# Input and forget gate columns with the weights stationary and the tokens moving

## What is computed

```python
h = rms_norm_2(x, mix_norm[l])
z = h @ w_in[l] + b_in[l]
a_q, a_k, a_v, m_q, m_k, m_v, m_o, m_i, m_f, g_pre = jnp.split(z, SPLIT_POINTS, axis=-1)
...
hm = mlstm_chunkwise(mq, mk, mv,
                     softcap(m_i.astype(jnp.float32)), softcap(m_f.astype(jnp.float32)))
```

## Time and profile before

| | us |
|---|---|
| median of 3 runs | 1102.63 |
| lowest, highest | 1102.37, 1106.66 |
| the profiled execution's own time | 1103.3 |
| its span, first to last instruction | 1101.6 |
| TensorE busy in it | 1040.7 (94%) |
| VectorE, ScalarE busy | 556.0 (50%), 428.2 (39%) |
| mean granted TensorE clock | 0.979 |

### The profile page before, as it was taken

One profiled execution on the slowest core, in us unless ns is written; L12 is line 12 of the kernel. 1 busy time (PEld: TensorE's weight loads), 2 busy tenths in 40 slices (PEclk: granted clock), 3 DMA queues, 4 the chain that ended last, 5 costly groups with the idle time before them and its releaser, 6 DMA issues.

```text
span 1101.6 us, 13370 instructions
## 1 busy us (share of the span) xinstructions
PE 1040.7 (94%) x5377; PEld 799.0 (73%) x5377; DVE 556.0 (50%) x844; ACT 428.2 (39%) x564; POOL 51.5 (5%) x57
## 2 busy tenths in 40 slices
PE   7997999999999999999999999978999999999997
PEld 6885886654444448778788899856788888877875
DVE  5577454222222255444445647587755655444443
ACT  4456232322222143443444444384344344444342
POOL 2430000000000000000000000010100000000000
PEclk9999899999999999999999999888999999999999
DMA  8872375999999957555555555311175636555540
GB/s 287 265 260 112 153 308 207 369 421 418 422 421 421 421 199 253 191 159 184 190 171 173 175 189 189 124 70 39 41 246 191 191 115 221 180 190 156 187 152 39
DMA packets 101821, 239.60 MB, mean 218 GB/s; under 512 B 11666, under 2 KB 56810, under 8 KB 86282
## 3 DMA queue, kind: packets, MB, share of 16 engines
q1 hardware_dynamic: 99850, 229.05, 57.3%
q0 software_dynamic: 1920, 9.85, 2.6%
HBM read 237.81 MB, written 3.43 MB: 219 GB/s over the span
## 4 chain that ended last, share of the span: by engine, by line
PE 79%; DVE 7%; ACT 6%; issue 5%; POOL 1%; DVEq 0%; ACTq 0%; POOLq 0%
PE banks L1038 18%; PE banks L1040 17%; PE banks L1039 17%; PE banks L1268 8%; PE banks L1293 5%; ACT weights_hi L666 4%; PE banks L1248 3%; PE banks L1277 3%; DVE stage L2025 1%; PE banks L1045 1%; PE banks L1183 1%; PE banks L1392 1%; PE banks L1055 1%; PE banks L1152 1%; ACT stage L744 1%
## 5 line engine op out<-in xcount | busy, mean ns | idle before, releaser
L1687 DVE TENSOR_TENSOR weights_lo<-raw_weights,weights_hi 128x2048 fp32r<-128x2048 f32 x116 | 265.8, 2292 | 216.8 <-ACT weights_hi L666 216.6
L666 ACT ACTIVATE weights_hi<-raw_weights 128x2048 fp32r<-128x2048 f32 x116 | 221.8, 1913 | 175.4 <-PE banks L1040 160.0
L1038 PE MATMUL banks<-weights_hi,normed_T_hi 128*128 128x512 f32 (+1 forms) x624 | 247.6, 397 | 9.8 <-DVE stage L2025 7.5
L1040 PE MATMUL banks<-weights_hi,normed_T_lo 128*128 128x512 f32 (+1 forms) x624 | 243.0, 389 | 0.0
L1039 PE MATMUL banks<-weights_lo,normed_T_hi 128*128 128x512 f32 (+1 forms) x624 | 242.1, 388 | 0.0
L1038 PEld LDWEIGHTS banks<-weights_hi,normed_T_hi 128*128 128x128 f32 x624 | 118.1, 189 | 40.8 <-DVE stage L2025 13.3
L1040 PEld LDWEIGHTS banks<-weights_hi,normed_T_lo 128*128 128x128 f32 x624 | 117.7, 189 | 25.0
L1039 PEld LDWEIGHTS banks<-weights_lo,normed_T_hi 128*128 128x128 f32 x624 | 117.9, 189 | 22.6
L1038 PE MATMUL banks<-weights_hi,ffn_hidden_T_hi 128*128 128x512 f32 x160 | 62.4, 390 | 0.0
L1040 PE MATMUL banks<-weights_hi,ffn_hidden_T_lo 128*128 128x512 f32 x160 | 62.3, 389 | 0.0
L1039 PE MATMUL banks<-weights_lo,ffn_hidden_T_hi 128*128 128x512 f32 x160 | 62.2, 389 | 0.0
(11 more groups left out here) (356 smaller groups left out, 1673.0 us busy)
## 6 DMA issues: line engine op xcount, KB each, us to landing
raw_weights<-in_w_in SPq DMA_DIRECT2D x38, 1024.0 KB, 5.0
raw_weights<-in_ffn_w_gate SPq DMA_DIRECT2D x44, 512.0 KB, 3.9
raw_weights<-in_ffn_w_up SPq DMA_DIRECT2D x44, 512.0 KB, 4.9
raw_weights<-in_ffn_w_down SPq DMA_DIRECT2D x22, 1024.0 KB, 4.7
stage<-in_w_down SPq DMA_DIRECT2D x14, 1024.0 KB, 11.8
expert_weights<-in_w_gate SPq DMA_DIRECT2D x12, 1024.0 KB, 11.0
expert_weights<-in_w_up SPq DMA_DIRECT2D x12, 1024.0 KB, 13.6
expert_weights<-in_w_down SPq DMA_DIRECT2D x12, 1024.0 KB, 14.5
```

The source lines that it names most:

```text
L666: ins = eng.activation(w_hi[:, slot, :], raw, ACT.Copy)
L1038: eng.matmul(dst, x[0], w[0], start=first_one, stop=False)
L1040: return eng.matmul(dst, x[1], w[0], start=False, stop=last_one)
L1687: ins = eng.tensor_tensor(w_lo[:, slot, :], raw, w_hi[:, slot, :], ALU.subtract)
```

## The change

The high and low parts of the gate weights are put side by side in one tile, `w_if_both`, 32 columns. For each of the eight slices those 32 columns are stationary, and the 256 tokens of `hT` move, once the high and once the low part: 16 products into partitions 0 to 31 of bank 2 (`PS[0:32, 2, 0:SEQ]`). The result is transposed, with gates in partitions and tokens in columns, and high and low weights apart. VectorE copies it to `gate_cols` (`gate_columns`). Four small float32 products bring it back to tokens in partitions and add the two parts: for each token tile, 128 columns of `gate_cols` are stationary and 16 columns of the identity move, twice. They stand on TensorE in group 7, first piece, between token tile 0 and tile 1. `aT` now shares the tile `gate_cols`, and `cols_copied` counts both copies. On VectorE `take(9)` moves behind the second `feed` of group 7.

```diff
-        w_if_parts = [sb(f"w_if_{x}", [P, KT, 16], F32R) for x in ("hi", "lo")]
+        w_if_both = sb("w_if_hi_lo", [P, KT, 32], F32R)
+        w_if_parts = [w_if_both[:, :, 0:16], w_if_both[:, :, 16:32]]
@@
-        aT = sb("a_rows", [MLSTM_HEADS, SEQ])
+        gate_cols = sb("gate_columns", [32, SEQ])
+        aT = gate_cols[0:MLSTM_HEADS, :]
@@ z_bank
-                return PS[:, 2 + units_of[g].index(n), :]
+                return PS[:, 3, units_of[g].index(n) * 16:]
@@ TensorE, for each unit n of group g, piece kh
+                        if (g, kh, i) == (7, 0, 1):
+
+                            eng.wait_ge(cols_copied, 1)
+                            for m in units_of[9]:
+                                for part in range(2):
+                                    mm = eng.matmul(z_bank(m)[:, 0:16], gate_cols[:, Z[m][2] * P:(Z[m][2] + 1) * P],
+                                                    ident[0:32, 16 * part:16 * part + 16], start=(part == 0), stop=(part == 1))
+                                mm.then_inc(z_unit, 1)
@@ TensorE, behind group 6
-                    for n in units_of[9]:
-                        i = Z[n][2]
-                        for k in range(KT):
-                            mm = product(z_bank(n)[:, 0:16], both(hT, lambda h: h[:, k, i * P:(i + 1) * P]),
-                                         both(w_if_parts, lambda w: w[:, k, :]), k == 0, k == KT - 1)
-                        mm.then_inc(z_unit, 1)
+                    for k in range(KT):
+                        for part in range(2):
+                            mm = eng.matmul(PS[0:32, 2, 0:SEQ], w_if_both[:, k, :], hT[part][:, k, :],
+                                            start=(k == 0 and part == 0), stop=(k == KT - 1 and part == 1))
+                    mm.then_inc(z_unit, 1)
@@
-            eng.wait_ge(a_copied, 1)
+            eng.wait_ge(cols_copied, 2)
@@ VectorE
-                        eng.wait_ge(z_unit, i + 1)
@@
                 if g == 7:
-                    take(9)
+                    eng.wait_ge(z_unit, 1)
+                    eng.tensor_copy(gate_cols[:, :], PS[0:32, 2, 0:SEQ]).then_inc(cols_copied, 1)
                 feed(z_piece(g) + 1)
                 if g == 7:
+                    eng.wait_ge(z_unit, 1 + TILES)
+                    take(9)
@@
-            eng.tensor_copy(aT[:, :], PS[0:8, 5, 0:SEQ]).then_inc(a_copied, 1)
+            eng.tensor_copy(aT[:, :], PS[0:8, 5, 0:SEQ]).then_inc(cols_copied, 1)
```

More of the change, by code:

```diff
@@ L302, in two_blocks @@
         gates_exp, gates_u, gates_ready = sem("gates_exp"), sem("gates_u"), sem("gates_ready")
-        cum_ps, a_ready, a_ps, a_copied = sem("cum_ps"), sem("a_ready"), sem("a_ps"), sem("a_copied")
+        cum_ps, a_ready, a_ps, cols_copied = sem("cum_ps"), sem("a_ready"), sem("a_ps"), sem("cols_copied")
         sink_exp, sig_done = sem("sink_exp"), sem("sig_done")
```

## The result

| | median of 20, us | lowest | ratio to before, with 95% interval |
|---|---|---|---|
| before | 1105.21 | 1099.62 | |
| changed | 1109.74 | 1104.92 | 1.0033 (1.0019 to 1.0046) |

What follows compares the result with a forecast made beforehand. TensorE, on 79% of the chain that ended last, was taken to bound the kernel. At group 8's end, +0.2 us at full clock and +2.0 us for low clock made +2.2: 1102.63 + 2.2 = 1104.8 us, range 1101.2 to 1108.

Steps and rivals of the forecast that it cites:

- The new wait: After 12 wide products of group 7, TensorE stands 5.9 us until VectorE's copy of the gate columns is done.
- the copy's start: On VectorE, behind the weight split and two bias adds, the copy of the gate columns starts at 699.96.
- the 16 products: On TensorE, the new gate products with 256 moving columns take 16 x 0.12 = 1.92 us.
- Late gate adds: Tile 9's adds stand behind one more split on VectorE; priced at nothing, 0.9 us if the slack were gone.
- The direction of the shift: At the end of group 8 the changed kernel is slower, by +2.2 us.
- (c): Faster by more than 0.5%: copy reached before TensorE needs it, 1097.1 us, or fewer low-clock stretches behind 720; chance 0.06.
- Turning products: Four small float32 products on TensorE after the copy, bringing gates back to tokens in partitions: 0.94 us at full clock.
- the clock after the wait: Once TensorE resumes in group 7, 4.3 us run at half clock, losing 0.47 each: +2.0 us.
- the far end: Upper end for low clock once TensorE resumes: 6.8 us, the longest single stretch in the rows, losing 3.2 us.
- The base: Median time of the whole kernel before the change, taken as 1102.63 us, to which +2.2 us was added.
- (a): TensorE stands for the copy, but the clock stays up or is back by 700.4: 1102.8 us; chance 0.12.
- (b): Slower by more than 0.5%: extra low-clock stretches between 720 and 773 lose 4.7 us, 1109.5 us; chance 0.10.

Runs made afterwards that it cites:

- copy first: The changed kernel with VectorE's copy of the gate columns moved ahead of the weight split and the two bias adds; ratio to before 0.9931.
- Wait only: The changed kernel with the wait kept between the tiles and only the four small float32 products moved to the start of group 8; ratio to before 1.0008.
- first and late: The changed kernel with the copy ahead of the weight split and the four small float32 products at the start of group 7's second piece; ratio to before 0.9946.

## Why the prediction was wrong

**Right, by its own steps.** The new wait: 5.9 us forecast, 5.80 measured; the copy's start at 699.96 + 1.95 = 701.91, as measured; its length 0.41, measured 0.40; the 16 products 1.92, measured 1.84. Late gate adds at no price: no wait of TensorE for weights in that place. The direction of the shift (+2.2) and the class, no change by the bound of 0.5%, also held; so did rival (c)'s price, 5.5 us if the copy comes before TensorE needs it, which "copy first" gave as 5.4.

**Turning products.** The row of three small float32 products gave 0.94 us for four at full clock; "copy first" shows 0.99, in eight records. The Trainium skill ("FP8 and Floating Point Precision", TensorE Precision Notes) says that true FP32 takes four passes; at a narrow pitch of 0.11 us for each, an estimate, the four products would take 1.8 us at full clock. The trace does not bear out that price, as the row of before already said. It does not refute the four passes either: a filler product with 128 moving columns leaves two records too, and takes 0.23 us (24 of them in 5.52) where one with 16 takes 0.25. How many passes stand behind a record, no run shows.

**The term that failed is the clock after the wait.** It was put at 4.3 us of low clock, the middle of 3.4 and 5.2, worth 2.0 us; it was 6.8, 6.9 and 6.4 us in three profiles, worth 3.2 in the first. Neither row that I took the middle of has this kernel's work behind a stop: the 3.4 stand behind a stop but are score products, the 5.2 are wide products behind the narrow ones, with no stop. The middle had no other reason. I counted the turning products as ordinary work (at a low clock "double, which is inside the term below"), although the same text named narrow products as what stood before the fall of the clock. "Wait only" shows the difference: without them 3.0 to 3.8 us, near the lower of the two rows. The moment at which the clock falls in the wait, which the forecast left open, counts as well: in the third profile it fell late, and 6.4 of its 6.8 us of low clock lay behind the wait. The value that I gave as the far end, 6.8, was the right one. With it the sum is +0.2 + 3.2 = +3.4, against +3.56 measured in the local stretch.

**The base failed too, and it is what put the measurement outside the range.** The forecast was 1102.63 + 2.2, and 1102.63 is a median of three executions. Over 20 executions the kernel before has 1105.21: 2.6 us of the 4.9 that the forecast was short by. The clock term is 1.2 of the rest; put right alone, it would have given 1106.0, still 3.7 short. Of the last 1.1 us, 0.9 are no step of the sum: the two medians stand that much further apart (4.5) than the ratio gives (3.6). The sign was there to be seen: one of the three was 1106.66. The range treated this as rounding (1107.6 to 1108), where it should have been a term of its own. The measured median, 1109.74, lies 1.7 us above the range's end; with the base of 20 executions the same steps would have given 1107.4 and a range of 1103.8 to 1110.6, which holds it.

**The rivals.** (a), no low clock, is refuted by three profiles. (b), at least 7 us more of low clock behind 720, did not come about at that size. In the two profiles compared, the low stretches behind the local stretch last 6.8, 3.4, 6.8 and 6.8 us in the changed kernel and 6.8, 3.4, 3.4 and 6.8 before, and from the first score product to the end it is 381.1 us against 379.9. That is the 1.3 us left over above. It is not shown to belong to the change: this last part took 377.5 us in "copy first", 380.8 in "first and late" and 382.3 in the third profile of the changed kernel, so it scatters by more than that. (c) needed another order, which an experiment gave it.

## What to carry to other kernels

When a step is moved to another engine and back, read where the link lands in that engine's queue, and put the consumer behind enough other work: here the same edit is worth -0.6 to -0.7% or +0.3%, by the place of one copy or of four small products. A row of 48 short, narrow products cost twice, its own time and the clock of what followed; set apart, six at a time between wide ones, they cost only once, and directly behind a stop the four turning products went with a longer low stretch. If a stop can't be avoided, filler products in it can be worth their while: they gave 3.2 us here. Before a forecast is hung on a median, look whether the runs behind it fall into groups.

## What the runs showed of the chip

The executions of the kernel before fall into two groups about 5 us apart: of the 20, 9 lie between 1101.6 and 1104.2, 10 between 1106.2 and 1108.2, and one at 1099.6. The other versions scatter as widely, though not always in two groups; "copy first" ran from 1092.5 to 1101.0. Two profiles of the changed kernel, with spans of 1108.4 and 1104.1, show one such difference far ahead of the change, in the first block's attention. The windows view of the longer one:

```profile
109.00:116.00 7.00, 5.65 (x33) 0.70 0.00 0
116.00:120.00 4.00, 3.31 (x18) 0.66 0.01 2
```

and of the shorter one:

```profile
109.00:116.00 7.00, 5.93 (x51) 1.00 0.00 1
116.00:120.00 4.00, 4.00 (x39) 1.00 0.01 4
```

The clock was low in that stage in one and full in the other. The second group of L1185 starts at 119.86 in the one and 115.59 in the other, 4.3 us apart, and the gate products 5.3 us apart (691.82, 686.57). The spans differ by 4.3. That the two groups of run times are this is likely, but it was not shown for each run.

That 32 stationary columns would run as fast as 128 was expected; they ran a little faster, a pitch of 0.115 (1.84 us for 16) against 0.12 in the earlier trace rows.
